# The low part of every fourth feed-forward weight block by a ScalarE negation and an adding DMA

## The reference

```python
D_FF = -(-8 * D_MODEL // (3 * 256)) * 256        # 5632
h = rms_norm(x, norm_ffn[l])
x = x + (jax.nn.silu(h @ w_ffn_gate[l]) * (h @ w_ffn_up[l])) @ w_ffn_down[l]
```

## Time and profile before

| | |
|---|---|
| median of three runs | 1967.16 us |
| span of the profiled execution | 1965.2 us |
| time outside the span (the difference to the median) | 1.96 us |
| TensorE matmul busy | 1958.2 us, 100% of the span |
| VectorE busy | 1374.1 us, 70% |
| ScalarE busy | 1049.7 us, 53% |
| GpSimd busy | 0.2 us |
| mean rate of the DMA engines | 180 GB/s |
| VectorE making WL (L2076) | 649 x 1222 ns = 787.6 us with part of it overlapped |
| ScalarE making WH (L1564) | 649 x 1056 ns = 682.0 us likewise |

### The profile page before, as it was taken

One profiled execution on the slowest core, in us unless ns is written; L12 is line 12 of the kernel. 1 busy time (PEld: TensorE's weight loads), 2 busy tenths in 40 slices (PEclk: granted clock), 3 DMA queues, 4 the chain that ended last, 5 costly groups with the idle time before them and its releaser, 6 DMA issues.

```text
span 1965.2 us, 28011 instructions
## 1 busy us (share of the span) xinstructions
PE 1958.2 (100%) x11018; PEld 1699.3 (86%) x11018; DVE 1374.1 (70%) x2101; ACT 1049.7 (53%) x1640; POOL 0.2 (0%) x4
## 2 busy tenths in 40 slices
PE   9999999999999999999999999999999999999999
PEld 7889988988888888898888888888888888888887
DVE  6756777987557676898688877777764456666543
ACT  5645555665456754575566655544444344444433
POOL 0000000000000000000000000000000000000000
PEclk9999999999999999999999999999999999999999
DMA  8554335555533455555534345555555455555552
GB/s 324 181 185 171 129 108 189 175 193 193 190 139 143 177 193 193 176 180 204 213 115 158 110 169 196 189 189 184 190 192 193 176 209 185 184 190 192 193 214 108
DMA packets 51719, 353.39 MB, mean 180 GB/s; under 512 B 5652, under 2 KB 7196, under 8 KB 9860
## 3 DMA queue, kind: packets, MB, share of 16 engines
q1 hardware_dynamic: 50016, 348.84, 49.3%
q10 hardware_dynamic: 1572, 2.75, 0.4%
HBM read 349.47 MB, written 2.11 MB: 179 GB/s over the span
## 4 chain that ended last, share of the span: by engine, by line
PE 94%; DVE 4%; ACT 1%; issue 1%; ACTq 0%; DVEq 0%
PE bank L1137 94%; DVE WL L2076 2%; DVE AR L2253 0%; ACT WH L1564 0%; DVE AR L2366 0%; DVE XP L2249 0%; DVE AR L2363 0%; DVE XP L2351 0%; PE bank L1278 0%; DVE AR L2242 0%; DVE AR L2277 0%; DVE AR L2276 0%; ACT XP L1695 0%; ACT L1577 0%; PE bank L1517 0%
## 5 line engine op out<-in xcount | busy, mean ns | idle before, releaser
L2076 DVE TENSOR_TENSOR WL<-raw,WH 128x1024 fp32r<-128x1024 f32 x649 | 787.6, 1222 | 319.5 <-ACT WH L1564 311.8
L1564 ACT ACTIVATE WH<-raw 128x1024 fp32r<-128x1024 f32 x649 | 682.0, 1056 | 448.2 <-PE bank L1137 442.2
L1137 PE MATMUL bank<-XP,WH 128*128 128x512 f32 (+2 forms) x2096 | 668.3, 393 | 0.4 <-DVE XP L2351 0.2
L1137 PEld LDWEIGHTS bank<-XP,WL 128*128 128x128 f32 x2016 | 378.1, 188 | 81.2 <-issue 0.7
L1137 PE MATMUL bank<-FP,WH 128*128 128x512 f32 x1408 | 443.2, 395 | 0.0
L1137 PE MATMUL bank<-XP,WL 128*128 128x256 f32 (+1 forms) x2016 | 409.5, 279 | 0.1
L1137 PEld LDWEIGHTS bank<-XP,WH 128*128 128x128 f32 (+1 forms) x2096 | 328.7, 188 | 7.7 <-issue 1.4
L1137 PEld LDWEIGHTS bank<-FP,WL 128*128 128x128 f32 x1408 | 264.5, 188 | 62.1
L1137 PE MATMUL bank<-FP,WL 128*128 128x256 f32 x1408 | 277.3, 278 | 0.0
L1137 PE MATMUL bank<-WH,AP 128*128 128x512 f32 x704 | 217.2, 389 | 1.0 <-issue 1.0
L1137 PEld LDWEIGHTS bank<-FP,WH 128*128 128x128 f32 x1408 | 214.9, 189 | 0.5
(11 more groups left out here) (325 smaller groups left out, 1713.4 us busy)
## 6 DMA issues: line engine op xcount, KB each, us to landing
raw<-in_W SPq DMA_DIRECT2D x326, 1024.0 KB, 4.8
out<-XT ACTq DMA_DIRECT2D x8, 256.0 KB, 2.1
raw<-in_W SPq DMA_DIRECT2D x3, 512.0 KB, 6.7
X<-in_x SPq DMA_DIRECT2D x3, 512.0 KB, 12.7
AR<-rv SPq DMA_DIRECT2D x1, 1024.0 KB, 5.9
cst<-in_cst SPq DMA_DIRECT2D x1, 899.5 KB, 11.4
raw<-in_W SPq DMA_DIRECT2D x2, 256.0 KB, 4.2
AR<-in_sgu SPq DMA_DIRECT2D x1, 512.0 KB, 5.6
```

The costliest lines, as they stand in the source:

```text
L1137: return pe.matmul(o, lhsT, rhs, start=start, stop=stop)
L1564: ac.activation(w_slot(WH, s), raw_half(hf), ACT.Copy).then_inc(s_hi, 1)
L2076: tt(w_slot(WL, s), raw_half(pl.half_of[s]), w_slot(WH, s).bitcast(F32), ALU.subtract).then_inc(s_lo, 1)
```

## The change

In the feed-forward part, halves s with s % 4 == 1 (from 389 to 649) are split differently. There are 66 of them: 22 in each of ff0 and ff1, 11 in each of dn0 and dn1; all use the same slot of WH and WL. ScalarE, having made WH, waits for its own result and writes -WH to WL. GpSimd then issues a DMA from SBUF to SBUF that adds the raw half to WL. VectorE leaves these halves out. TensorE (and SyncE, ahead of its next load into the raw buffer) waits for the DMA's semaphore `s_dlo` in place of `s_lo`. The remaining edits fold semaphores together: `s_warm` into `s_vchain`, and `s_hot` and `s_sgu` into `s_late`.

```diff
+        ffn0 = next(pl.split_no[hf] for (hf, _), t in zip(pl.places, pl.tiles) if t[0] == "w_ffn_gate_2")
+        by_dma = [s for s in range(ffn0, len(pl.split_no)) if s % 4 == 1]
+
+        def low_ready(s):
+
+            if s in by_dma:
+                return s_dlo, 16 * (by_dma.index(s) + 1)
+            return s_lo, parts_split(s) - sum(d < s for d in by_dma)
...
-                    pe.wait_ge(s_lo, parts_split(s))
+                    pe.wait_ge(*low_ready(s))
...
                 ac.activation(w_slot(WH, s), raw_half(hf), ACT.Copy).then_inc(s_hi, 1)
+                if s in by_dma:
+                    ac.wait_ge(s_hi, parts_split(s))
+                    ac.activation(w_slot(WL, s), w_slot(WH, s).bitcast(F32), ACT.Copy, scale=-1.0).then_inc(s_neg, 1)
...
             def lo(s):
 
+                if s in by_dma:
+                    return
...
-                            sp.wait_ge(s_lo, parts_split(pl.split_no[hf]))
+                            sp.wait_ge(*low_ready(pl.split_no[hf]))
...
+        def pool_program():
+            for i, s in enumerate(by_dma):
+                if i:
+                    po.wait_ge(s_dlo, 16 * i)
+                po.wait_ge(s_neg, i + 1)
+                po.dma_start(w_slot(WL, s), raw_half(pl.half_of[s]), accum_op=ALU.add).then_inc(s_dlo, 16)
...
-            pe.wait_ge(s_warm, 1)
+            pe.wait_ge(s_vchain, 1)
...
-            dv.memset(mu_acc[:, :], 0.0).then_inc(s_warm, 1)
+            chain(dv.memset(mu_acc[:, :], 0.0))
...
-                    dv.wait_ge(s_sgu, 32)
+                    dv.wait_ge(s_late, 48)
```

More of the change, by code:

```diff
@@ L800, in sem @@
             return ctx.enter_context(nc.semaphore(name))
-        pe, dv, ac, sp = nc.tensor, nc.vector, nc.scalar, nc.sync
+        pe, dv, ac, sp, po = nc.tensor, nc.vector, nc.scalar, nc.sync, nc.gpsimd
         pl = plan()
@@ L1008, in build @@
         s_hi, s_lo, s_proj = sem("s_hi"), sem("s_lo"), sem("s_proj")
+        s_neg, s_dlo = sem("s_neg"), sem("s_dlo")
         s_half = sem("s_half")
@@ L1016, in build @@
         s_raw0a, s_raw0b, s_raw1b = sem("s_raw0a"), sem("s_raw0b"), sem("s_raw1b")
-        s_warm = sem("s_warm")
-        s_cst, s_rv, s_bt, s_e8, s_hot, s_sgu, s_fin = (
-            sem(n) for n in ("s_cst", "s_rv", "s_bt", "s_e8", "s_hot", "s_sgu", "s_fin"))
+        s_cst, s_rv, s_bt, s_e8, s_late, s_fin = (
+            sem(n) for n in ("s_cst", "s_rv", "s_bt", "s_e8", "s_late", "s_fin"))
         s_xh, s_xl, s_ang, s_trig = sem("s_xh"), sem("s_xl"), sem("s_ang"), sem("s_trig")
@@ L1386, in pe_program @@
                     take(5)
-                    pe.wait_ge(s_hot, 16)
+                    pe.wait_ge(s_late, 16)
                     mm(bank[5][0:8, 0:383], P("table", 32), hot[0:32, 0:383], True, True).then_inc(s_band, 1)
@@ L1879, in act_program @@
                     ac.wait_ge(*outed("p1", AHEAD - 1))
-                    ac.dma_start(hot[0:32, :], dr["late"][0:32, 0:766]).then_inc(s_hot, 16)
+                    ac.dma_start(hot[0:32, :], dr["late"][0:32, 0:766]).then_inc(s_late, 16)
                 elif what == "nsa gates":
@@ L2559, in dve_program @@
                     dv.wait_ge(s_band, 1)
-                    dv.wait_ge(s_hot, 16)
+                    dv.wait_ge(s_late, 16)
                     tt(rv, bank[5][0:8, 0:383], hot[0:8, 383:766], ALU.add).then_inc(s_rvt, 1)
@@ L2909, in sync_program @@
                         sp.wait_ge(s_rsP, 1)
-                        sp.dma_start(sgw, dr["sgu"][:, 0:1024]).then_inc(s_sgu, 16)
-                        sp.dma_start(sgb[:, :], dr["sgu"][:, 1024:1536]).then_inc(s_sgu, 16)
+                        sp.dma_start(sgw, dr["sgu"][:, 0:1024]).then_inc(s_late, 16)
+                        sp.dma_start(sgb[:, :], dr["sgu"][:, 1024:1536]).then_inc(s_late, 16)
             sp.wait_ge(s_fin, 16 * 8)
+        def pool_program():
[4 more added lines that the diff above has]
+                po.dma_start(w_slot(WL, s), raw_half(pl.half_of[s]), accum_op=ALU.add).then_inc(s_dlo, 16)
         sync_program()
+        pool_program()
         act_program()
```

## The result

The changed kernel takes 2001.37 us, the median of four runs (1995.23 to 2004.66), against 1966.99 us, the median of four runs of the kernel before. The ratio is 1.0169 (95% interval 1.0157 to 1.0181): 34 us slower. The forecast was slower, 1984.5 us; the time is in the range, and the excess is twice the 17.3 us that I summed. The span of the profiled execution is 2000.7 us, 35.5 us over that of before.

What follows compares the result with a forecast made beforehand. TensorE was taken to bound the kernel; stalls of 44 x 0.32 + 22 x 0.145 = 17.3 us gave a span of 1982.5, and with 1.96 us outside it 1984.5 us. The range was 1964 to 2090 us.

Steps and rivals of the forecast that it cites:

- What bounds the kernel, and what the relief of VectorE is worth: TensorE bounds, busy 1958.2 of 1965.2 us; removing 80.9 us of VectorE subtractions gains at most 1.04 us, taken as nothing.
- How long the transfer may take: Time from GpSimd's issue to landing before TensorE needs WL: 5.67 us in ff, 5.47 us in dn.
- f: Adding DMA's time from issue to first data: taken as 1.2 us, bounds 0.9 to 3 us.
- W: Adding DMA's time with data: taken as 3.6 us, reads 2.4 then write 1.2; bounds 1.2 to 6.2 us.
- signs of being wrong: Negation waits long for the copy, software issue over 2 us, or adding DMA's data under 3 or over 4.5 us.
- my own formula: TensorE's stall per half: (W - 2.96) / 2 = 0.32 us in ff, (W - 3.31) / 2 = 0.145 us in dn.
- the transfer fits: Rival, chance 0.34: W up to 2.96 us and f up to 2.1 us give no stall; time stays 1967 us.
- The load in flight: The next unit's weight load shares the DMA engines with the addition: 2.08 - f left in ff, 1.53 - f in dn.
- The clock: TensorE's stalls are short, so its granted clock stays at full speed, 1.00, as at the 1 us gap.
- The sum: Stalls at 44 ff halves of 0.32 us and 22 dn halves of 0.145 us: 17.3 us in all.
- SyncE and the DMA share: SyncE's later wait stays hidden with 7 us to spare; DMA share rises from 0.53 to 0.65 to 0.8, not a bound.

Runs made afterwards that it cites:

- e7: Changed kernel with the negation made first, straight from raw, and weight loads held until the adding DMA has landed: 1970.53 us, ratio 1.0012.
- e1: Changed kernel with the adding DMA taken out; VectorE adds raw to WL, ScalarE's negations stay: 1967.65 us, ratio 1.0000.
- e10: Changed kernel with the 66 DMAs copying the raw half over WL in place of adding to it: 1985.44 us (one run).
- e2: Changed kernel with SyncE holding the weight load that would be in flight until the adding DMA has landed: 1975.67 us, ratio 1.0041.
- e4: Changed kernel with weight loads held so that two are issued shortly ahead of each adding DMA, at 65 halves: 2341.88 us (one run).
- e8: Kernel before, with ten stops of TensorE in ff0 and ff1, each waiting for one small GpSimd DMA; no adding DMA: 2003.02 us, ratio 1.0183.
- e3: Changed kernel with ScalarE making -WH first, straight from raw, and WH after it, so GpSimd can issue sooner: 1993.26 us, ratio 1.0132.
- e9: Kernel before, with ten stops of TensorE, each waiting for two small GpSimd DMAs in a row; no adding DMA: 2042.72 us, ratio 1.0384.

## Why the prediction was right or wrong

- **What bounds the kernel, and what the relief of VectorE is worth.** Right: TensorE did everything without idling, and 80 us less on VectorE gave nothing, not even in e7, where hardly a stop is left. e1 shows it from ScalarE's side too, with that engine's 70 us more at no cost.
- **How long the transfer may take.** The border was right in kind, and 0.53 us too wide. The negation ended where I had put it (1410.28 + 1.06 = 1411.34, 2.16 us after the copy's start), but GpSimd starts 0.53 us later (1411.87). Counted from GpSimd's start, 5.2 us are allowed in ff and 5.0 in dn. The twelve landings of 5.6 us and more are those that stop TensorE; those up to 5.4 us show no stop. But I read the border at two steady places and took it for all 66. Near the start of ff0 ScalarE's copy comes late, TensorE is there 2.9 us after the issue, and that one place costs 3.1 us.
- **f.** I took 1.2 us; it is 0.53 + 1.43 = 1.96 us from the end of the negation, inside the bounds.
- **W.** I took 3.6 us, reads and write in turn; 2.77 us is what was measured, nearer to both reads at the full rate with the write beside them (2.4). Data in under 3 us was one of the signs of being wrong that I had named, and this was the step on which the verdict was to hang: by my own formula 2.77 is the case "the transfer fits", with no loss at all. A copy has data for 1.46 us (e10), so the ratio is 1.9. It agrees with the reading of the Trainium skill in "Collectives: The Full Stack", section "The bandwidth ceiling: the fold count and why AG ≠ RS ≠ AR", which puts it down to the second read and not to the addition; e10 takes away both at once, so no run here tells the two apart. The 6.15 us that the Trainium skill gives in "DMA: Bandwidth & Descriptors", section "Measured (HBM→SBUF, 128 partitions, SWDGE, issued from GpSimd)", for 1 MB from HBM are not what 1 MB of reads within SBUF takes here, 2.77 us.
- **The load in flight.** This step failed. I had one steady load whose remains share the engines, and so 66 equal stalls of 0.32 and 0.145 us. The steady load costs 0.3 us of landing and no stall. The loss sits where loads are issued 0.2 to 1.8 us ahead of the addition, and there the addition waits out most of the load: e2 takes this away and 26 us with it, e4 makes it the rule. Of the 21.4 us of stops, 11.3 are behind VectorE's waits for a block of a down product, 8.2 near the start of ff0, dn0 and dn1 (2.4 of these are the late copy), and 1.9 elsewhere. The trace of before had the hint: its loads, 5.6 us apart in the steady turn, are issued 10.9 and then 2.3 us apart behind dn0 (at about 1589, 1600 and 1602). I built the sum on one steady turn and never looked at the turns between sections.
- **The clock.** This step failed too. I had stalls too short for it; the stops were 12 and up to 4.5 us long, and half clock behind five of them added 9.3 us, a quarter of the loss. The 1.04 us gap in the earlier trace rows, with the clock at 1.00, showed what a gap of 1 us does and nothing about one of 3 us; e8 does.
- **The sum.** 17.3 us was forecast, 34 measured. The sign was right, the size half, and the reason for the size not the one I gave: too much for W, nothing for the transitions, the late copy and the clock. With W as measured my formula gives 1967 us, so that the direction came out, and the time fell in the range, was luck: one error made up for the others.
- **The rival "the transfer fits".** Its condition for dn was not worked out: by the formula, W = 2.96 with f = 2.1 gives 0.22 us there and not 0. It decided nothing.
- **SyncE and the DMA share.** Right: no wait for raw, and a share of 0.71 where I had 0.65 to 0.8.

Not settled by an experiment is what makes one landing in ten 0.6 to 1.5 us late without a fresh load ahead; the packets point to instruction packets and outputs beside it (e2). The cost is small: what e2 leaves is 8 us, the late copy included, and e7 2.6 us. Open too is why the addition waits while most of a fresh load moves.

## What to carry to other kernels

Before a step is moved to a DMA that the bounding engine waits for, compare its landing with the slack at the worst place, not in the steady turn: look where another engine's wait holds releases back, for there the large loads went out bunched and the small transfer stood behind them, and where the engine that feeds the transfer is itself behind with other work. A transfer that has to be on time is protected by holding bulk loads until it has landed (e2), not by issuing it sooner (e3). If the engine relieved is not the one that bounds, there is nothing to win that could pay for the risk.

## What the runs showed of the hardware

- A DMA issued by GpSimd that adds 0.5 MB from SBUF to SBUF: GpSimd starts 0.53 us after its semaphore, data from 1.43 us, 2.77 us with data, landing 4.5 us after the start when nothing else is in flight. The same as a copy: data from 1.10 us, 1.46 us with data, landing 2.9 us (e10).
- An adding DMA behind a 1 MiB load issued 0.2 to 1.8 us earlier by SyncE, on another queue, waits for most of that load: landings of 5.9 to 9.8 us, and the load's own in 5.2 to 7.8 us. With the load 2.5 us ahead it is 4.8 us in most turns.
- Ten stops of TensorE of 1.8 to 3.3 us, 26.4 us in all, made the kernel 35.1 us slower (e8), and ten of 3.8 to 8.1 us, 54.2 us in all, 74.8 us (e9): 1.3 to 1.4 times their length. The larger part of the surcharge is half clock behind them.
